# Thirty of the 32 query tiles of the last gate stage as three products of rounded parts

## The chip, the cores and the metric

The kernel runs on one core of a Trainium2 chip. The metric is device time in microseconds (us) of the whole program. Engines are named as in the profile: PE is TensorE's matmuls and PEld its weight loads, DVE is VectorE, ACT is ScalarE, POOL is GpSimd, SP is SyncE, which issues most of the DMA loads. A line such as L1227 is a line of the kernel before.

## The reference, cut to what matters

The program is a hybrid block (a gated delta rule, latent attention, a feed-forward part) followed by a second block with two layers of "product-key experts". In the last of these the 256 image tokens go through this:

```python
q = (hb @ w_q).reshape(PEER_BLOCK, PEER_HEADS, 2, PEER_DHALF)      # 1024 -> 8 heads x 2 x 256
s = jnp.einsum("nhkd,hkmd->nhkm", q, sub_keys)                     # 128 scores for each half
s_half, i_half = lax.top_k(s, PEER_TOPK)                           # 16 best of each half
cand = s_half[:, :, 0, :, None] + s_half[:, :, 1, None, :]         # 256 sums
top_s, top_c = lax.top_k(cand.reshape(..., 256), PEER_TOPK)        # 16 best pairs of a head
g = jax.nn.softmax(top_s, axis=-1)                                 # gates, then 16384 experts
```

`hb` is the input (1024 features by 256 tokens), `w_q` has 4096 output features: 32 tiles of 128, four for each head. All is float32.

## The kernel before

**Products.** TensorE multiplies float32 data in two ways here. A plain float32 product shows in the trace as two matmul records for each instruction of the program. The other way uses the type float32r: each operand is split into a high part (a copy rounded to that type) and a low part (the value less its high part), and three products high x high, high x low and low x high are summed in PSUM. Each of those is one record. The function `parted` (L682 to L692) does so for two earlier stages: ScalarE copies a 128x1024 tile of weights from the ring to a high buffer, VectorE subtracts it to make the low buffer (L2038), and the tensor engine multiplies 3 x 8 blocks (L688). The last gate stage before the change uses plain float32 products (L1227).

**The ring.** SyncE streams all weights through four SBUF slots of 128x1024 floats (512 KB each) in one fixed order. It refills a slot when the first matmul of a later slot has raised `slot_begun`; four loads at most are ahead. A consumer waits on `slot_loaded0` to `slot_loaded3`.

**The last gate stage** is `peer_last`, written once for each engine. Its order on each is as follows.
- VectorE scales the input (L2531), ScalarE shifts it (L1722) into `HT`, VectorE splits `HT` into high and low parts `HR` (L2542, L2543), which the expert sweep behind the stage needs.
- TensorE makes tile t of the queries into PSUM bank t % 2, eight blocks of 128x128 by 256 tokens (L1227). ScalarE copies it to SBUF (L1487 is the copy helper) and raises `lin_free`. After tile 4, 8, ... and at the end the tensor engine makes the scores of one head, `keys(h)`, 8 matmuls (L1212). `keys(h)` waits until VectorE has taken the scores of head h-2 (`key_scores_used`).
- VectorE takes each head's scores through `choice`: top 16 of each half (L2376 to L2380), the sums of pairs (L2393), top 16 of them, and the decoding of the indices (L2404 to L2418). After head 7 come the softmax (ScalarE L1770, VectorE L2451 to L2453), whose end raises `chosen`.
- Behind `keys(7)` TensorE works ahead on the first products of the expert sweep (L1025). It turns the choice (L1145) when `chosen` is raised, and then builds the gates in 32 groups (L1136) with VectorE (L2549 to L2553), ScalarE (L1777) and further work ahead (L1025) beside it. The expert sweep (L1045, L1047, L1059) follows.
- GpSimd waits for the split input, stores the residual to HBM (`park`, L420), waits for that, copies `HT` into the place of the residual (`unpark`, L425), waits, and has no more to do until near the end of the sweep.

Of the kernel before, what the change touches and what calls it, by code (L numbers as in the profile page):

```python
# [70 lines left out]
for _name, _w in (("in", 56), ("uq", 6), ("kn", 2), ("v", 2), ("o_gdn", 8), ("o_mla", 8), ("out", 8),  # L71
# [2 lines left out]
    SEGS[_name] = (_n, _w)  # L74
    _n += _w
NSLOTS = _n


def row_at(q):
# [63 lines left out]
def build(nc, io):  # L143
    ctx = ExitStack()
    with ctx:
# [23 lines left out]
        with nc.sbuf_tensor("arena_front", [P, 8192], F32):  # L169
            with nc.sbuf_tensor("wk_even", [P, 2, KD_, S], F32R) as t:  # L170
                WKL0, WKH0 = t[:, 0], t[:, 1]
                with nc.sbuf_tensor("wk_gap_a", [P, 2560], F32):
                    with nc.sbuf_tensor("wk_odd_low", [P, KD_, S], F32R) as t:
                        WKL1 = t[:, :, :]
                        with nc.sbuf_tensor("wk_gap_b", [P, 4608], F32):
                            with nc.sbuf_tensor("wk_odd_high", [P, KD_, S], F32R) as t:
                                WKH1 = t[:, :, :]
                                with nc.sbuf_tensor("text_low_a", [P, 4, S], F32R) as t:
                                    TLA = t[:, :, :]
                                    with nc.sbuf_tensor("wk_gap_c", [P, 2816], F32):  # L180
                                        with nc.sbuf_tensor("text_low_b", [P, 4, S], F32R) as t:
                                            TLB = t[:, :, :]
                                            with nc.sbuf_tensor("wk_gap_d", [P, 256], F32):
                                                with nc.sbuf_tensor("text_high", [P, KD_, S], F32R) as t:
                                                    TH = t[:, :, :]
# [227 lines left out]
        def _(pool):  # L413
# [4 lines left out]
            def park(dst, src, n):  # L418

                pool.dma_start(dst, src).then_inc(sem("x_parked"), 16)  # L420
                pool.wait_ge(sem("x_parked"), 16 * n)
# [98 lines left out]
            batch(io["cm"], 15)  # L520
            pool.wait_ge(sem("x_back"), 16 * (NH + 5))
            pool.wait_ge(sem("input_parts"), 4)
            park(parked[:, :, image], X[:, :, image], 5)
            unpark(INPUT, HT, NH + 6)
            pool.wait_ge(sem("coef_ready"), 3 * NEXP - 8)
            unpark(XT, parked[:, :, image], NH + 7)

# [79 lines left out]
        def _(pe):  # L607
# [3 lines left out]
            def arrived(w):  # L611
                pe.wait_ge(sem(f"slot_loaded{w % RING}"), 16 * (w // RING + 1))
# [420 lines left out]
            def split_experts(p):  # L1033

                n0, s0, e = NEXP * p, STEADY[p], AHEAD[p]
                if p:
                    L.take("input_parts")

                def up(j, b, first=False):

                    if not first:
                        pe.wait_ge(sem("sum_ready"), j + (s0 - e - 1))
                    pe.wait_ge(sem("u_low"), j + (s0 - e + 1))
                    for k in range(8):
                        mm(bank(b), SPL[b][:, 0, 0, P * k:P * k + P], HR[:, k, :, :], start=(k == 0), stop=False,  # L1045
                           skip_group_check=True)
                        last = mm(bank(b)[:, 0:S], SPL[b][:, 0, 1, P * k:P * k + P], HR[:, k, 0, :], start=False,  # L1047
                                  stop=(k == 7), skip_group_check=True)
                    last.then_inc(sem("up_ready"), 1)

                def down(j, b, first=False, opening=False):

                    parts = v_parts(j, b, opening)
                    pe.wait_ge(sem("coef_ready"), j + (n0 + 1))
                    pe.wait_ge(sem("v_low"), j + (n0 + 1))
                    for i in range(2):
                        for c, v in ((0, 0), (0, 1), (1, 0)):
                            for f in range(2):
                                last = mm(bank(2 + 2 * i + f), CFR[:, b, c, P * i:P * i + P],  # L1059
                                          parts[:, v, 512 * f:512 * f + 512],  # L1060
                                          start=(first and c == 0 and v == 0), stop=False, skip_group_check=True)
                    last.then_inc(sem("coef_used"), 1)

                if e:
                    pe.wait_ge(sem("gelu_done"), n0 + 10)
                    pe.wait_ge(sem("gates_evacuated"), n0 // 4 + 32)
                    for j in range(e):
                        if j == e - 1:
                            up(e, 0, True)
                        down(j, j % 2, j == 0, True)  # L1070
                    up(e + 1, 1, True)
                    down(e, 0)
                else:
                    up(0, 0, True)
                    up(1, 1, True)
                    pe.wait_ge(sem("gates_evacuated"), n0 // 4 + 32)
                    down(0, 0, True)
                with pe.Fori(0, (NEXP - 2 - e) // 2) as i:
                    for b in range(2):
                        up(i * 2 + (e + b + 2), b)  # L1080
                        down(i * 2 + (e + b + 1), 1 - b)
                down(NEXP - 1, 1)
# [116 lines left out]
            def peer_last():  # L1199

                l0 = L.lin

                def keys(h):

                    pe.wait_ge(sem("lin_free"), l0 + 4 * h + 4)
                    if h >= 2:
                        L.take("key_scores_used")
                    arrived(L.slots)
                    for k in range(2):
                        for i in range(2):  # L1210
                            for d in range(2):
                                last = mm(bank(2 + 4 * (h % 2) + i)[:, P * k:P * k + P],  # L1212
                                          QT[:, 4 * h + 2 * k + d, P * i:P * i + P],
                                          ring[:, L.slots % RING, P * (2 * k + d):P * (2 * k + d) + P],
                                          start=(k == 0 and d == 0), stop=(d == 1), skip_group_check=True)
                                if k == 0 and i == 0 and d == 0:
                                    last.then_inc(sem("slot_begun"), 1)
                    L.slots += 1
                    L.mark(last, "key_scores")

                for t in range(4 * NH):
                    pe.wait_ge(sem("lin_free"), l0 + max(t - 1, 0))
                    arrived(L.slots)
                    for k in range(8):
                        if t == 0:
                            L.take("inputs_shifted")
                        last = mm(bank(t % 2)[:, 0:S], ring[:, L.slots % RING, k * P:k * P + P], HT[:, k, :],  # L1227
                                  start=(k == 0), stop=(k == 7))
                        if k == 0:
                            last.then_inc(sem("slot_begun"), 1)  # L1230
                    last.then_inc(sem("lin_ready"), 1)
                    L.slots += 1
                    if t and t % 4 == 0:
                        keys(t // 4 - 1)
                keys(NH - 1)
                L.lin += 4 * NH
                beside = up_ahead(2)
                fill(beside, 32)
                for _ in range(2):
                    L.take("key_scores_used")  # L1240
                fill(beside, 12)
                turn_choice(KK)
                fill(beside, 9)
                L.take("chosen_evacuated")
                for n in range(32):
                    build(64 + n, n % 2, n < 2)
                    fill(beside, 1 if n % 3 == 2 else 2 if n < 31 else 8)
                sweep(2)
                turn_sums()
                L.take("acc_evacuated")  # L1250
                L.take("acc_evacuated")
# [232 lines left out]
        def _(act):  # L1484
# [244 lines left out]

            def queries():  # L1730

                def query(t, b, i=None):

                    n = L.lin + b + 1
                    act.wait_ge(sem("lin_ready"), n if i is None else i * 2 + n)
                    copy(QT[:, t, :], bank(b)[:, 0:S]).then_inc(sem("lin_free"), 1)

                query(0, 0)
                query(1, 1)
                with act.Fori(1, 2 * NH) as i:  # L1740
                    for b in range(2):
                        query(i * 2 + b, b, i)
                L.lin += 4 * NH
                act.wait_ge(sem("lin_free"), L.lin)

# [1226 lines left out]
```

## Time and profile before

| | us |
|---|---|
| median of 3 runs (4019.35 to 4029.62) | 4026.69 |
| the profiled execution | 4029.86 |
| its span, first to last instruction | 4027.9 |
| query tiles and first seven heads' scores | 3091.8 to 3217.0 |
| PE busy in the span | 3850.7 (96%) |
| DVE, ACT, POOL busy in the span | 2844.6, 1578.8, 88.1 |

The profile is of one execution. Its page has busy times by engine, the chain that ended last and the costliest groups; the trace behind it answers questions on one stretch, line or engine. A row of the timeline gives the start, the time that the instruction or the merged run of instructions took, the engine, line, operation and operands, and in brackets how long the engine was idle before it and what released it.

### The profile page before, as it was taken

To read this page: it belongs to the slowest core of one execution; us is meant where nothing else is said; L and a number is where in the kernel's file an instruction comes from. 1 tells how busy PE (TensorE), PEld (TensorE's weight loads), DVE (VectorE), ACT (ScalarE), POOL (GpSimd) and SP (SyncE) were. 2 spreads that over 40 slices of the span, in tenths; PEclk is the share of its full clock that TensorE was granted. 3 is DMA by queue.
4 is the path that set the end of the run, shared out by engine and by line. 5 is a ranking of instruction groups with operands and counts; after the bars stand their busy time and mean duration, and the time that the engine had idled before them with its cause. 6 is when DMAs were issued, how large, how long until landed. Compare 5 with 4: busy or idle time off the path is not lost.

```text
span 4027.9 us, 61202 instructions
## 1 busy us (share of the span) xinstructions
PE 3850.7 (96%) x21266; PEld 3190.8 (79%) x21266; DVE 2844.6 (71%) x5160; ACT 1578.8 (39%) x2416; POOL 88.1 (2%) x101
## 2 busy tenths in 40 slices
PE   7899899899999999999999999999969999999998
PEld 7697789554796888888888888888747888888887
DVE  6342356697598789999987777777562997777776
ACT  5201043132218544444475444444322084444443
POOL 0000000000000000000000000000400000000000
PEclk9899999899998999999999999999979999999999
DMA  5213255467424566666625666666765525666664
GB/s 191 63 48 106 93 174 168 161 224 236 141 96 135 178 196 191 195 191 190 198 89 162 188 188 188 189 190 193 174 208 168 168 68 184 189 190 188 188 188 145
DMA packets 203772, 666.51 MB, mean 165 GB/s; under 512 B 35920, under 2 KB 46176, under 8 KB 202480
## 3 DMA queue, kind: packets, MB, share of 16 engines
q1 hardware_dynamic: 166816, 602.71, 48.3%
q0 software_dynamic: 12496, 52.53, 4.2%
q10 hardware_dynamic: 24320, 9.37, 0.9%
q8 instruction: 91, 1.49, 0.2%
q14 instruction: 49, 0.40, 0.0%
HBM read 637.34 MB, written 26.15 MB: 165 GB/s over the span
## 4 chain that ended last, share of the span: by engine, by line
PE 91%; DVE 6%; DMA 2%; ACT 1%; issue 1%; SPq 0%; DVEq 0%; ACTq 0%; POOLq 0%
PE psum L1059 26%; PE psum L1045 17%; PE psum L1047 8%; PE psum L634 6%; PE psum L688 4%; PE psum L1136 4%; PE psum L712 4%; PE psum L1330 3%; PE psum L1227 3%; PE psum L1125 2%; PE psum L933 1%; PE psum L1025 1%; PE psum L1104 1%; DMA ring<-in_w 1%; PE psum L1400 1%
## 5 line engine op out<-in xcount | busy, mean ns | idle before, releaser
L1059 PE MATMUL psum<-rows_split_odd,coef_split 128*128 128x512 f32 x2400 | 590.9, 396 | 4.5 <-DVE rows_split_odd L2464 3.6
L1059 PE MATMUL psum<-rows_split,coef_split 128*128 128x512 f32 x2208 | 532.0, 390 | 0.3 <-issue 0.3
L2469 DVE TENSOR_REDUCE work<-psum 128x256 f32<-128x512 f32 x360 | 249.1, 692 | 400.6 <-PE psum L1047 399.5
L1059 PEld LDWEIGHTS psum<-rows_split_odd,coef_split 128*128 128x128 f32 x2400 | 437.9, 188 | 106.6 <-issue 6.7
L1045 PE MATMUL psum<-input_split,rows_split 128*128 128x512 f32 x1440 | 514.0, 397 | 1.2 <-DVE rows_split L2464 1.2
L1045 PE MATMUL psum<-input_split,rows_split_odd 128*128 128x512 f32 x1440 | 510.0, 393 | 0.0
L1680 ACT ACTIVATE work<-work 128x256 f32<-128x256 f32 x360 | 150.8, 419 | 875.6 <-DVE work L2469 875.6
L2464 DVE TENSOR_TENSOR rows_split_odd<-ring,rows_split_odd 128x1024 fp32r<-128x1024 f32 x380 | 462.6, 1218 | 5.9 <-ACT rows_split_odd L1487 5.9
L1059 PEld LDWEIGHTS psum<-rows_split,coef_split 128*128 128x128 f32 x2208 | 402.1, 188 | 81.4 <-issue 0.9
L1487 ACT ACTIVATE rows_split_odd<-ring 128x1024 fp32r<-128x1024 f32 x380 | 400.4, 1055 | 157.5 <-PE psum L1059 154.6
L2464 DVE TENSOR_TENSOR rows_split<-ring,rows_split 128x1024 fp32r<-128x1024 f32 x364 | 443.1, 1217 | 5.3 <-ACT rows_split L1487 5.3
L1487 ACT ACTIVATE rows_split<-ring 128x1024 fp32r<-128x1024 f32 x364 | 383.5, 1054 | 128.2 <-PE psum L1059 125.7
L1047 PE MATMUL psum<-input_split,rows_split_odd 128*128 128x256 f32 x1440 | 405.2, 281 | 0.0
L1047 PE MATMUL psum<-input_split,rows_split 128*128 128x256 f32 x1440 | 403.9, 280 | 0.0
L1487 ACT ACTIVATE arena<-psum 128x1024 f32<-128x1024 f32 (+6 forms) x209 | 176.9, 852 | 391.3 <-PE psum L1227 110.6
L1045 PEld LDWEIGHTS psum<-input_split,rows_split 128*128 128x128 f32 x1440 | 270.5, 188 | 66.1 <-ACT arena L1487 1.4
L1045 PEld LDWEIGHTS psum<-input_split,rows_split_odd 128*128 128x128 f32 x1440 | 270.4, 188 | 61.8
L1047 PEld LDWEIGHTS psum<-input_split,rows_split_odd 128*128 128x128 f32 x1440 | 271.5, 189 | 8.0
L1047 PEld LDWEIGHTS psum<-input_split,rows_split 128*128 128x128 f32 x1440 | 271.6, 189 | 6.9
L634 PE MATMUL psum<-arena,ring 128*128 128x256 f32 (+1 forms) x992 | 248.1, 409 | 6.5 <-DVE arena L2207 2.4
L634 PEld LDWEIGHTS psum<-arena,ring 128*128 128x128 f32 x992 | 189.0, 191 | 59.7 <-issue 28.4
L1136 PEld LDWEIGHTS psum<-work 128*128 128x128 f32 x1536 | 182.5, 194 | 49.7 <-issue 31.3
(447 smaller groups left out, 5296.2 us busy)
## 6 DMA issues: line engine op xcount, KB each, us to landing
ring<-in_u SPq DMA_DIRECT2D x384, 512.0 KB, 3.6
ring<-in_v SPq DMA_DIRECT2D x384, 512.0 KB, 3.5
ring<-in_w SPq DMA_DIRECT2D x372, 512.0 KB, 3.6
scratch_inj<-stage ACTq DMA_DIRECT2D x16, 512.0 KB, 5.5
arena<-scratch_inj POOLq DMA_DIRECT2D x7, 1024.0 KB, 7.7
scratch_cm<-work POOLq DMA_DIRECT2D x8, 512.0 KB, 6.2
scratch_cm<-arena POOLq DMA_DIRECT2D x8, 512.0 KB, 6.3
arena<-scratch_parked POOLq DMA_DIRECT2D x4, 1024.0 KB, 8.1
```

What stands on the lines that cost most here:

```text
L634: last = mm(bank(t % 2)[0:m, 0:n], ring[:, (w0 + s // 8) % RING, (s % 8) * P:(s % 8) * P + m], rhs[:, k, 0:n], start=(k == 0), stop=(k == ...
L688: last = mm(bank(t % 2)[:, 0:S], UPR[:, t % 3, w, P * k:P * k + P], UPI[:, k, x, :], start=(k == 0 and w == 0 and x == 0), stop=(k == 7 an ...
L712: ins = mm(bank(t % 2)[:, 0:S], ring[:, (w0 + s // 8) % RING, (s % 8) * P:(s % 8) * P + P], rhs[:, k, 0:S], start=(k == 0), stop=(k == kt ...
L1045: mm(bank(b), SPL[b][:, 0, 0, P * k:P * k + P], HR[:, k, :, :], start=(k == 0), stop=False, skip_group_check=True)
L1047: last = mm(bank(b)[:, 0:S], SPL[b][:, 0, 1, P * k:P * k + P], HR[:, k, 0, :], start=False, stop=(k == 7), skip_group_check=True)
L1059: last = mm(bank(2 + 2 * i + f), CFR[:, b, c, P * i:P * i + P], parts[:, v, 512 * f:512 * f + 512], start=(first and c == 0 and v == 0), s ...
L1136: last = mm(PS(1024 * b + P * t, P), EB[:, b, t, :], EA[:, b, t, :], start=(t % 4 == 0), stop=True, skip_group_check=True)
L1227: last = mm(bank(t % 2)[:, 0:S], ring[:, L.slots % RING, k * P:k * P + P], HT[:, k, :], start=(k == 0), stop=(k == 7))
L1487: copy = lambda o, i: f(o, i, ACT.Copy)
L1680: f(AC[:, b, :], AC[:, b, :], ACT.Gelu_apprx_tanh).then_inc(sem("gelu_done"), 1)
L2464: tt(parts[:, 1, :], ring[:, w % RING, :], parts[:, 0, :].bitcast(F32), ALU.subtract)\
L2469: dve.tensor_reduce(AC[:, b, :], bank(b).rearrange("p (x t) -> p t x", x=2), AX, ALU.add)\
```

## The change

Tiles 0 and 1 (`PLAIN` = 2) stay plain. For tiles 2 to 31 ScalarE copies the ring slot to the high half of one of three buffers `QW` (in regions of the arena that this stage does not use), GpSimd subtracts it from the slot to make the low half, and TensorE multiplies three times eight blocks with the split input `HR`. The high copy of tile t + 2 stands on ScalarE ahead of the copy of tile t out of PSUM; with three buffers it waits until tile t - 1 is done. TensorE waits for `input_parts` ahead of tile 2. On GpSimd the first two subtractions stand between the start of `park` and the wait for it, and the other 28 behind the start of `unpark`.

```diff
+QUERY_PARTS = QT_ - PLAIN + 1 + FT - PLAIN + 1 - PLAIN
+def query_slot(t):
+    return 4 * NEXP + SEGS["q1"][0] + t + max(0, (t - 1) // 4)
+def query_ring(t):
+    return query_slot(t) % RING
+def query_count(t):
+    return 16 * (query_slot(t) // RING + 1)
...
 # GpSimd
-            park(parked[:, :, image], X[:, :, image], 5)
-            unpark(INPUT, HT, NH + 6)
+            def query_low(t):
+                pool.wait_ge(sem("parts_high"), QUERY_PARTS + t + 1)
+                w = QW[t % 3]
+                pool.tensor_tensor(w[:, 1, :], ring[:, query_ring(t), :], w[:, 0, :].bitcast(F32), ALU.subtract)\
+                    .then_inc(sem("parts_low"), 1)
+            pool.dma_start(parked[:, :, image], X[:, :, image]).then_inc(sem("x_parked"), 16)
+            for t in range(PLAIN, 4):
+                query_low(t)
+            pool.wait_ge(sem("x_parked"), 80)
+            pool.dma_start(INPUT, HT).then_inc(sem("x_back"), 16)
+            for t in range(4, 4 * NH):
+                query_low(t)
+            pool.wait_ge(sem("x_back"), 16 * (NH + 6))
...
 # TensorE, peer_last
                 for t in range(4 * NH):
                     pe.wait_ge(sem("lin_free"), l0 + max(t - 1, 0))
-                    arrived(L.slots)
+                    if t >= PLAIN:
+                        pe.wait_ge(sem("parts_low"), QUERY_PARTS + t + 1)
+                    else:
+                        arrived(L.slots)
+                    if t == PLAIN:
+                        L.take("input_parts")
                     for k in range(8):
...
-                        last = mm(bank(t % 2)[:, 0:S], ring[:, L.slots % RING, k * P:k * P + P], HT[:, k, :],
-                                  start=(k == 0), stop=(k == 7))
+                        for w, x in ((0, 0), (0, 1), (1, 0)) if t >= PLAIN else ((0, 0),):
+                            first = k == 0 and w == 0 and x == 0
...
+                                last = mm(bank(t % 2)[:, 0:S], QW[t % 3][:, w, block], HR[:, k, x, :], start=first,
+                                          stop=(k == 7 and w == 1))
...
 # ScalarE, queries
+                def query_high(t):
+                    act.wait_ge(sem(f"slot_loaded{query_ring(t)}"), query_count(t))
+                    if t >= PLAIN + 3:
+                        act.wait_ge(sem("lin_ready"), L.lin + t - 2)
+                    copy(QW[t % 3][:, 0, :], ring[:, query_ring(t), :]).then_inc(sem("parts_high"), 1)
+                for t in range(PLAIN, PLAIN + 2):
+                    query_high(t)
+                for t in range(4 * NH):
+                    if PLAIN + 2 <= t + 2 < 4 * NH and t >= PLAIN:
+                        query_high(t + 2)
+                    act.wait_ge(sem("lin_ready"), L.lin + t + 1)
+                    copy(QT[:, t, :], bank(t % 2)[:, 0:S]).then_inc(sem("lin_free"), 1)
```

## Rows read from the trace of the kernel before

**Rows 1.** The page: shares of the span in the chain that ended last.

```profile
PE 91%; DVE 6%; DMA 2%; ACT 1%; issue 1%; SPq 0%; DVEq 0%; ACTq 0%; POOLq 0%
```

**Rows 2.** Timeline of ACT: copies of query tiles 0, 30 and 31.

```profile
3097.88 0.38 ACT L1487 ACTIVATE arena<-psum 128x256 f32<-128x256 f32 x1 [2.80 <-PE psum L1227]
...
3214.08 0.38 ACT L1487 ACTIVATE arena<-psum 128x256 f32 x1 [3.07 <-PE psum L1227]
3217.54 0.38 ACT L1487 ACTIVATE arena<-psum 128x256 f32 x1 [3.07 <-PE psum L1227]
```

**Rows 3.** Waits from 3080 to 3230: us in total, times, longest.

```profile
DVE arena L2376 <- PE psum L1212: 17.9, 7, 14.9
```

**Rows 4.** Timeline: first head's choice on DVE, and the scores on PE.

```profile
3113.54 0.89 DVE L2376 MAX8 arena<-psum 128x8 f32<-128x128 f32 x4 [14.88 <-PE psum L1212]
...
3118.94 0.69 DVE L2393 TENSOR_TENSOR arena<-arena 128x512 f32<-128x512 f32 x1
...
3124.01 0.18 DVE L2404 TENSOR_SCALAR arena<-arena 128x32 uint32<-128x32 uint32 x1
...
3124.91 1.22 DVE L2413 TENSOR_TENSOR arena<-arena,small 128x1024 f32<-128x1024 f32 x1
3126.16 1.22 DVE L2416 TENSOR_TENSOR arena<-arena 128x1024 f32<-128x1024 f32 x1
3127.42 1.22 DVE L2418 TENSOR_REDUCE arena<-arena 128x64 f32<-128x1024 f32 x1
3129.14 0.89 DVE L2376 MAX8 arena<-psum 128x8 f32<-128x128 f32 x4 [0.50 <-PE psum L1212]
...
3111.49 1.95 PE L1212 MATMUL psum<-ring,arena 128*128 128x128 f32 x16
```

**Rows 5.** Timeline: the end of the choice, and PE until it turns it.

```profile
3219.86 19.16 PE L1025 MATMUL psum<-X,ring 128*128 128x256 f32 x88
...
3222.30 0.89 DVE L2376 MAX8 arena<-psum 128x8 f32<-128x128 f32 x4
...
3238.97 0.42 DVE L2453 TENSOR_TENSOR arena<-arena,tail 128x256 f32<-128x256 f32 x1
...
3239.45 0.87 PE L1145 MATMUL psum<-small,arena 128*128 128x128 f32 x6 [0.43 <-DVE arena L2453]
```

**Rows 6.** Timeline of an earlier stage in three products (L688).

```profile
60.61 1.06 ACT L1487 ACTIVATE up_rows<-ring 128x1024 fp32r<-128x1024 f32 x1
...
62.31 0.47 ACT L1548 ACTIVATE arena<-psum,small 128x256 f32<-128x256 f32 x1 [0.64 <-PE psum L688]
...
65.19 0.47 ACT L1548 ACTIVATE arena<-psum,small 128x256 f32<-128x256 f32 x1 [0.70 <-PE psum L688]
```

**Rows 7.** Timeline of POOL and DVE where POOL's part begins.

```profile
3096.37 2.29 DVE L2543 TENSOR_TENSOR input_split<-arena,input_split 128x2048 fp32r<-128x2048 f32 x1
...
3099.21 0.85 POOL L420 DMA_DIRECT2D scratch_parked<-X  x1 [102.64 <-DVE input_split L2543]
...
3106.35 0.57 POOL L425 DMA_DIRECT2D X<-arena  x1 [6.29 <-DMA scratch_parked<-X]
```

**Rows 8.** POOL's memset of a 128x1024 tile: duration ns min/median/max.

```profile
L436 POOL MEMSET arena<- x4: 951/951/1024, 244.3 to 281.6; 128x1024 f32 x4
```

**Rows 9.** DVE beside POOL's DMA issues (L493): lines, then the timeline.

```profile
L2746 DVE TENSOR_SCALAR work<-work x7: 195/196/796, 2845.7 to 2854.4; 128x64 f32<-128x64 f32 x7
L2740 DVE TENSOR_TENSOR work<-work,tail x7: 224/224/226, 2844.5 to 2853.3; 128x64 f32<-128x64 f32 x7
...
2852.09 7.99 POOL L493 DMA_DIRECT2D arena<-scratch_lags  x7 [10.96 <-issue]
...
2852.44 0.80 DVE L2746 TENSOR_SCALAR work<-work 128x64 f32<-128x64 f32 x1
```

**Rows 10.** Stretches, us: busy PE, PEld, DVE, ACT, POOL, clock, DMA share, GB/s.

```profile
3091.00:3095.00 4.00, 3.22 (x8) 2.63 (x9) 2.29 (x7) 3.97 (x8) 0.00 (x0) 0.50 0.20 30
...
3260.00:3300.00 40.00, 37.84 (x283) 34.21 (x283) 37.88 (x60) 40.00 (x104) 0.00 (x0) 1.00 0.13 40
```

More of the change, by code:

```diff
@@ L171, in build @@
                 WKL0, WKH0 = t[:, 0], t[:, 1]
+                QW = [t[:, n].rearrange("p a b -> p (a b)").rearrange("p (w c) -> p w c", w=2) for n in range(2)]
                 with nc.sbuf_tensor("wk_gap_a", [P, 2560], F32):
@@ L174, in build @@
                         WKL1 = t[:, :, :]
+                        QW.append(t.rearrange("p a b -> p (a b)").rearrange("p (w c) -> p w c", w=2))
                         with nc.sbuf_tensor("wk_gap_b", [P, 4608], F32):
@@ L1035, in split_experts @@
                 n0, s0, e = NEXP * p, STEADY[p], AHEAD[p]
-                if p:
+                if p == 1:
                     L.take("input_parts")
@@ L1222, in peer_last @@
                     pe.wait_ge(sem("lin_free"), l0 + max(t - 1, 0))
-                    arrived(L.slots)
+                    assert L.slots % RING == query_ring(t)
+                    if t >= PLAIN:
[4 more added lines that the diff above has]
+                        L.take("input_parts")
                     for k in range(8):
@@ L1226, in peer_last @@
                             L.take("inputs_shifted")
-                        last = mm(bank(t % 2)[:, 0:S], ring[:, L.slots % RING, k * P:k * P + P], HT[:, k, :],
-                                  start=(k == 0), stop=(k == 7))
-                        if k == 0:
-                            last.then_inc(sem("slot_begun"), 1)
+                        block = slice(k * P, k * P + P)
+                        for w, x in ((0, 0), (0, 1), (1, 0)) if t >= PLAIN else ((0, 0),):
+                            first = k == 0 and w == 0 and x == 0
+                            if t < PLAIN:
+                                last = mm(bank(t % 2)[:, 0:S], ring[:, L.slots % RING, block], HT[:, k, :],
+                                          start=(k == 0), stop=(k == 7))
+                            else:
+                                last = mm(bank(t % 2)[:, 0:S], QW[t % 3][:, w, block], HR[:, k, x, :], start=first,
+                                          stop=(k == 7 and w == 1))
+                            if first:
+                                last.then_inc(sem("slot_begun"), 1)
                     last.then_inc(sem("lin_ready"), 1)
@@ L1730, in queries @@
             def queries():
[L1732 to L1742, printed above, removed]
+                def query_high(t):
[10 more added lines that the diff above has]
+                    copy(QT[:, t, :], bank(t % 2)[:, 0:S]).then_inc(sem("lin_free"), 1)
                 L.lin += 4 * NH
```

## The prediction

> **What bounds the kernel now.** I read the page's chain first: PE holds 91% of it [rows 1], so TensorE bounds the program as a whole. That says nothing about one stage, so I then read the stage by its waits and its timeline.
>
> Queries on TensorE: the copies of tiles 30 and 31 start 3.46 us apart [rows 2], so a plain tile takes 3.46 us. A head is four tiles and the scores' 1.8 us. Choice on VectorE: the first head starts at 3113.54, the second at 3129.14 after 0.50 us of idling [rows 4]; one head's choice therefore takes 3128.64 - 3113.54 = 15.10 us, in a period of 15.60 us. VectorE's seven waits for scores sum to 17.9 us, the first of them 14.9 [rows 3]: from the first head to the last it idles 3.0 us. Both engines are full, and what the next stage waits for is `chosen`, the end of VectorE's chain: 3238.97 + 0.42 = 3239.39 [rows 5]. TensorE fills the time after its last query with 19.16 us of work ahead and is idle only 0.43 us before it turns the choice [rows 5]. So the stage ends by two chains that are almost equally long. TensorE's cannot shorten it by more than VectorE's allows, and VectorE's is (start of the first choice) + 7 x 15.10 + (last choice and softmax, 3239.39 - 3222.30 = 17.09) + waits.
>
> **What is saved on TensorE.** An earlier stage with the same 24 matmuls a tile has its copies 65.19 - 62.31 = 2.88 us apart [rows 6]. Thirty tiles x (3.46 - 2.88) = 17.4 us. A head becomes 4 x 2.88 + 1.9 = 13.45 us, shorter than VectorE's 15.10. So all but a little of the 17.4 us turns into idling of TensorE at the end of its work ahead. What can reach the next stage is the 3.0 us of VectorE's waits and whatever the first choice gains at its start.
>
> **GpSimd's subtraction.** No row shows it. Its memset of the same tile, one stream of data, takes 0.95 us [rows 8], the low bound. Two reads and one write, all in turn, would be 3 x 0.95 = 2.85, the high bound. Two streams would be 1.90; I take 2.25, between two and three. The Trainium skill (GPSIMD Engine Reference, "Performance versus the Vector engine") gives 4497 ns for twice the size, half of which is 2.25 by that page; no row here shows it. At 2.25 GpSimd keeps up with 2.88. ScalarE's high copy is 1.06 us [rows 6] beside a copy of 0.38 [rows 2], so ScalarE keeps up too. After tile n is done, copy and high copy give the low part of tile n + 3 about 1.8 us later, ready 4.05 us after tile n; TensorE wants it 5.76 us after. That stays hidden. SP's loads go at 2.88 us a slot in the earlier stage [rows 6], so the ring is no new wait.
>
> **The start.** Tile 0 ends at about 3097.8 [rows 2], tile 1 at 3101.3. GpSimd waits for the split input, 3096.37 + 2.29 = 3098.66, and for the issue at 3099.21 of 0.85 us [rows 7]. Subtraction 2 then ends at 3102.3, subtraction 3 at 3104.6. Now it waits for the parked residual: the next issue starts at 3106.35 and takes 0.57 [rows 7], so subtraction 4 runs from 3106.9 to 3109.2. Tile 2 runs 3102.3 to 3105.2, tile 3 to 3108.1, tile 4 from 3109.2 to 3112.1, where the first scores start; before they started at 3111.49 [rows 4]. The first choice starts 0.6 us later, at 3114.15. With subtractions of 0.95 the store's wait remains and it is 0.7 earlier; with 2.85, 1.2 later.
>
> **GpSimd and VectorE in each other's way.** This is the largest term. Row: a VectorE operation of 0.20 us with one SBUF input took 0.80 beside GpSimd's DMA issues [rows 9]. It started at 2852.44 and ended at 2853.24; the first of seven issues in 7.99 us (1.14 each) that began at 2852.09 ended at 2853.23. VectorE stood still until GpSimd's instruction was over. VectorE's operations with two SBUF inputs kept 0.22 us [rows 9], but GpSimd read no tensor there. The subtraction reads two. I take it that it and VectorE's operations with two SBUF inputs exclude each other as whole instructions, and that the small one-input ones (from L2404) are held as in rows 9. The low bound is nothing; the high bound is that each of the 25 subtractions after the first choice's start holds VectorE for its full length, 25 x 2.25 = 56 us.
>
> The Trainium skill (SBUF — State Buffer, "Who interferes with whom") says that a VectorE instruction with two SBUF inputs contends with a GpSimd instruction that reads SBUF, and that the later one blocks fully. By that rule the sum is the one below; by the 0.22 us row alone it would lose most of this term.
>
> In a choice the exposed operations are the sums at offset 5.40 (0.69 us) and a group from offset 10.47 to 13.84: four small ones and two of 1.22 [rows 4]. Place the subtractions at 1.8 us after each tile's end and count, times from 3100:
> - Choice 0 starts 14.15, sums wanted 19.55. Subtraction 8 holds 18.75 to 21.0: 1.45 lost. The group wants 26.05; subtraction 10 ends 26.75: 0.7. Subtraction 11, ready at 27.4, gets in between two operations: 2.25. In all 4.4.
> - Choice 1 starts 33.65. Sums meet subtraction 14: 1.2. Subtractions 16 and 17 get in between operations of the group: 4.5. In all 5.7.
> - Choice 2 starts 54.5: 1.55, 0.75 and 2.2, in all 4.5.
> - By now TensorE is so far ahead that `keys(5)` waits for VectorE, and subtractions come later: choice 3 loses 1.1, choice 4 0.25, the rest none, since subtraction 31 is done in choice 4.
>
> Sum 15.95, call it 16, with 6 to 26 as the range of this count. Choice 7 then ends at 3114.15 + 105.7 + 16 + 17.1 = 3253.0.
>
> **TensorE's clock.** TensorE would finish its work ahead near 3233 and idle some 20 us. At the stage's opening it had idled 4.14 us and then had 0.50 of the clock, 1.2 GHz for 2.4, until tile 0 was out: 3091 to 3095 at 0.50 [rows 10], first copy at 3097.88 [rows 2]. Turning the choice took 0.87 us at full clock [rows 5]. About 6.8 us at half rate lose 3.4; in the gate building TensorE is busy 37.84 of 40 us and ScalarE 40.00 [rows 10], so little is regained. I take 2.5, from 0 to 4.
>
> **Sum.** +0.6 start, -3.0 waits, +16 exclusion, +2.5 clock = +16.1 us. The profiled execution's own time is 4029.86 (span 4027.9 and 1.96 around it), so it becomes 4046. That execution lies 3.2 us above the median of 4026.69; on the median's scale the forecast is 4043. A measurement of this kernel tells about 0.3%, 12 us, from no change: the three runs spread over 10.
>
> **Rivals.**
> 1. No exclusion between the subtraction and VectorE. For it: the 0.22 us row [rows 9]. Against: there GpSimd read nothing. The sum is +0.6 - 3.0 + 2.5 = +0.1, at most 4.7 us faster if the start and clock cost nothing: 4027 (4022 to 4031). This is the case on the other side, not slower; it decides if L2393, L2413 and L2416 keep their starts and lengths.
> 2. Only the small one-input operations are held. For it: L2746's row. GpSimd is busy 9.0 of 13.45 us; a group meets it with 0.67 x 1.12 = 0.75 us, and 0.9 us of small operations let another in with 0.27 x 2.25 = 0.6. Five heads x 1.35 = 6.7; in all +6.8: 4034.
> 3. The subtraction is dearer than its high bound, say 4 us, or its first call is slow, and GpSimd sets the pace. 30 x 4.0 + 3101 + the store's wait of 2 = 3223 for subtraction 31, last scores 3228, chosen 3245 without any exclusion; with 16 to 25 us of exclusion it is 3265: +20 to +35, 4055. For it: no row prices it. Against: memset at 0.95.
> 4. TensorE's 17 us arrive in full: 4009. Against: VectorE's 15.10 a head, which nothing shortens.
>
> **Chances.** Forecast 0.55 (its own range +8 to +28, 4035 to 4055), rival 1 0.16, rival 2 0.10, rival 3 0.17, rival 4 0.02. Over 12 us slower: 0.43 of the forecast's 0.55 and 0.16 of rival 3, 0.59. Within 12 us: 0.15 + 0.12 + 0.10 + 0.01 = 0.38. Faster: 0.03. The range leaves out a tenth on each side: 4021, the end of rival 1, to 4063, into rival 3.
>
> **What would show it.** Right: 24 matmuls a tile and 2.88 us between copies while nothing blocks; GpSimd subtractions of about 2.25; first choice at about 3114; choices 0 to 2 of 19 to 21 us with L2393, L2404 or L2413, L2416 stretched or delayed by up to 2.25, the last two 15.1; TensorE idle about 20 us before L1145 and at half clock after it. Wrong: choices of 15.1 throughout (rival 1), only L2404 to L2410 stretched (2), tiles over 3.4 us apart from the start (3). The sizes hang on where the subtractions fall among VectorE's operations, and on who goes first when both wait.

## The result and the profile after

The changed kernel takes 4048.59 us (median of 6, 4037.39 to 4063.25), the kernel before 4023.02 in the same comparison (median of 6, 4016.83 to 4029.62). The ratio is 1.0064 with a 95% interval of 1.0050 to 1.0078: 26 us slower, 20 to 31 by the interval. The execution profiled is the longest of the six, with a span of 4061.3 us, 33.4 above the span before. Of these, 4.6 us lie ahead of the stage, in code that is the same in both: the stage opens (ScalarE's eight normalizations) at 3095.66 instead of 3091.03. In the nine profiled executions (before, after and the seven experiments) that opening moves from 3082 to 3096, and what lies behind the stage takes 692.6 to 694.3 us, so everything below is counted from the opening. The table is worked out from the timelines of both kernels.

| us from the stage's opening | before | after | difference |
|---|---|---|---|
| first choice starts on VectorE | 22.51 | 27.50 | +5.0 |
| seven periods from choice to choice | 108.76 | 130.14 | +21.4 |
| last choice and softmax, to `chosen` | 17.09 | 17.08 | 0 |
| `chosen` to the start of the next expert sweep | 94.28 | 96.66 | +2.4 |
| sum | 242.64 | 271.38 | +28.7 |

Lines of the changed kernel for those of before: MAX8 L2423 (L2376), sums L2440 (L2393), small operations L2451 to L2457 (L2404 to L2410), the two products and the reduction L2460, L2463, L2465 (L2413, L2416, L2418), scores L1243 (L1212), work ahead L1056 (L1025), turning the choice L1176 (L1145). New are the matmuls of three products L1271 and GpSimd's subtraction L545.

The page's chain of the changed kernel answers to [rows 1]: VectorE has two points more, TensorE three fewer.

```profile
PE 88%; DVE 8%; DMA 2%; ACT 1%; issue 1%; SPq 0%; DVEq 0%; ACTq 0%; POOLq 0%
```

The waits of the changed kernel from 3080 to 3300 (us in total, times, longest) answer to [rows 3]. `wk_even` and `wk_odd_low` are the buffers `QW` of the split weights.

```profile
ACT wk_even L1531 <- DMA ring<-in_w: 43.1, 20, 8.0
...
ACT wk_odd_low L1531 <- DMA ring<-in_w: 23.5, 9, 7.3
...
DVE arena L2423 <- PE psum L1243: 19.9, 1, 19.9
...
PE psum L1056 <- DVE arena L2440: 11.4, 1, 11.4
...
PE psum L1176 <- DVE arena L2500: 3.9, 1, 3.9
```

VectorE now waits for scores once, before its first choice; the other six waits of [rows 3], 3.0 us, are gone. New is that ScalarE waits for weights in the ring, 29 times.

The timeline of the changed kernel from the opening to the first choice, beside [rows 4] and [rows 7]:

```profile
3103.83 0.85 POOL L548 DMA_DIRECT2D scratch_parked<-X  x1 [104.30 <-DVE input_split L2590]
3104.72 2.41 POOL L545 TENSOR_TENSOR wk_odd_low<-ring,wk_odd_low 128x1024 fp32r<-128x1024 f32 x1
...
3110.69 0.59 POOL L552 DMA_DIRECT2D X<-arena  x1 [1.21 <-DMA scratch_parked<-X]
3111.30 2.40 POOL L545 TENSOR_TENSOR wk_even<-ring,wk_even 128x1024 fp32r<-128x1024 f32 x1
...
3113.85 3.10 PE L1271 MATMUL psum<-input_split,wk_even 128*128 128x256 f32 x24 [0.64 <-POOL wk_even L545]
3118.02 1.06 ACT L1531 ACTIVATE wk_odd_low<-ring 128x1024 fp32r<-128x1024 f32 x1 [7.26 <-DMA ring<-in_w]
3118.98 0.37 ACT L1531 ACTIVATE arena<-psum 128x256 f32<-128x256 f32 x1
...
3119.40 3.65 PE L1243 MATMUL psum<-ring,arena 128*128 128x128 f32 x16 [2.44 <-ACT arena L1531]
```

Read it from the end. The first scores started when ScalarE had copied out query tile 3 (3118.98). That copy stood behind the high copy of tile 5 (3118.02), which had waited 7.26 us for tile 5's weights. The loads of the ring, the 1 MB store of the residual (issued at 3103.83) and the 1 MB return (3110.69) are under way together here. The load of tile 5's weights was issued at 3110.64, just ahead of the return, and the two took this long from issue to landing (KB, us):

```profile
X<-arena POOLq DMA_DIRECT2D x1, 1024.0 KB, 7.6
ring<-in_w SPq DMA_DIRECT2D x1, 512.0 KB, 7.4
```

The start has a second part. TensorE had idled 2.44 us before the scores and made them with half the clock (the stretch from 3120 to 3122; columns as in [rows 10]):

```profile
3120.00:3122.00 2.00, 2.00 (x11) 2.00 (x11) 0.00 (x0) 0.89 (x2) 2.00 (x2) 0.50 0.35 43
```

They took 3.65 us for the 1.95 of [rows 4]. So of the +5.0 us, 3.3 are scores that start later against the opening (23.74 for 20.46) and 1.7 are scores made at the lower clock.

The timeline of the first choice after the change, against [rows 4]:

```profile
3127.88 2.40 POOL L545 TENSOR_TENSOR wk_odd_low<-ring,wk_odd_low 128x1024 fp32r<-128x1024 f32 x1 [0.34 <-ACT wk_odd_low L1531]
...
3128.56 2.26 DVE L2440 TENSOR_TENSOR arena<-arena 128x512 f32<-128x512 f32 x1
...
3134.10 4.83 POOL L545 TENSOR_TENSOR wk_even<-ring,wk_even 128x1024 fp32r<-128x1024 f32 x2 [3.83 <-ACT wk_even L1531]
...
3135.20 1.31 DVE L2451 TENSOR_SCALAR arena<-arena 128x32 uint32<-128x32 uint32 x1
...
3136.54 2.43 DVE L2453 TENSOR_SCALAR arena<-arena 128x32 uint32<-128x32 uint32 x1
...
3139.47 1.23 DVE L2460 TENSOR_TENSOR arena<-arena,small 128x1024 f32<-128x1024 f32 x1
3139.66 3.29 POOL L545 TENSOR_TENSOR wk_odd_low<-ring,wk_odd_low 128x1024 fp32r<-128x1024 f32 x1 [0.72 <-ACT wk_odd_low L1531]
...
3140.73 3.31 DVE L2463 TENSOR_TENSOR arena<-arena 128x1024 f32<-128x1024 f32 x1
...
3144.07 1.22 DVE L2465 TENSOR_REDUCE arena<-arena 128x64 f32<-128x1024 f32 x1
```

The sums (0.69 us in [rows 4]) were issued at 3128.56 and recorded until 3130.82; the subtraction that was already running ended at 3130.28. The two small operations ended at 3136.51 and 3138.97, which is the end of the first and of the second of the two subtractions from 3134.10 to 3138.93: the second subtraction got in between two VectorE operations that follow each other, and an operation of 0.18 us took 2.43. The subtraction at 3139.66 lasted 3.29 us instead of 2.40, since L2460 was running until 3140.70; then L2463, issued at 3140.73, had to wait for that subtraction to end (3142.95) and ended 1.1 us after it. So the recorded duration of a held operation holds its wait, and each engine holds the other. The reduction, 1.22 us beside a subtraction, was not held. Added up, choice 0 lost 1.57 + 1.13 + 2.25 + 2.08 = 7.0 us.

The lines of VectorE's operations after the change, 3085 to 3260 (ns min/median/max):

```profile
L2440 DVE TENSOR_TENSOR arena<-arena x8: 691/692/2836, 3128.6 to 3258.7; 128x512 f32<-128x512 f32 x8
...
L2453 DVE TENSOR_SCALAR arena<-arena x7: 181/181/2432, 3136.5 to 3248.9; 128x32 uint32<-128x32 uint32 x7
L2457 DVE CAST arena<-arena x7: 195/195/2385, 3139.2 to 3249.3; 128x64 f32<-128x64 uint32 x7
...
L2463 DVE TENSOR_TENSOR arena<-arena x7: 1224/3303/3310, 3140.7 to 3250.8; 128x1024 f32<-128x1024 f32 x7
L2465 DVE TENSOR_REDUCE arena<-arena x7: 1220/1220/1222, 3144.1 to 3252.0; 128x64 f32<-128x1024 f32 x7
```

By the groups' means over this stretch, the excess over the shortest duration is L2463 8.3 us, L2453 4.4, L2440 3.7, L2451 3.5, L2457 2.2, L2460 2.1: 24.2 us. That is all but 0.2 us of what the periods gained over 15.1 (22.16, 18.47, 21.42, 20.61, 17.22, 15.12, 15.14: 7.1, 3.4, 6.3, 5.5, 2.1, 0, 0).

The end of the stage after the change, on TensorE's timeline and in two stretches of 2 and 4 us (busy PE, PEld, DVE, ACT, POOL, clock, DMA share, GB/s), against [rows 5] and [rows 10]:

```profile
3232.78 15.29 PE L1056 MATMUL psum<-X,ring 128*128 128x256 f32 x64
3259.49 7.02 PE L1056 MATMUL psum<-X,ring 128*128 128x256 f32 x24 [11.42 <-DVE arena L2440]
3270.44 1.54 PE L1176 MATMUL psum<-small,arena 128*128 128x128 f32 x6 [3.93 <-DVE arena L2500]
...
3270.00:3272.00 2.00, 1.56 (x7) 1.56 (x8) 0.38 (x1) 0.00 (x0) 0.00 (x0) 0.50 0.00 0
3272.00:3276.00 4.00, 4.00 (x10) 3.14 (x10) 3.88 (x6) 1.86 (x6) 0.00 (x0) 0.50 0.01 2
```

TensorE idled 11.42 + 3.93 = 15.4 us before it turned the choice, and did that and the next 4 us at half clock: 1.54 us for what took 0.87 at full clock [rows 5].

### The profile page after: what moved, and what is told of

Same layout as the page of the kernel before. It is cut to its first block, busy times and chain, and to the rows that moved or that the text cites. A ratio compares the mean times of both kernels' runs of the same rounds, so it can differ in the third digit from the quotient of the medians.

```text
span 4061.3 us, 61679 instructions
## 1 busy us (share of the span) xinstructions
PE 3854.5 (95%) x21506; PEld 3203.2 (79%) x21506; DVE 2867.7 (71%) x5160; ACT 1609.9 (40%) x2446; POOL 164.8 (4%) x131
## 4 chain that ended last, share of the span: by engine, by line
PE 88%; DVE 8%; DMA 2%; ACT 1%; issue 1%; SPq 0%; DVEq 0%; ACTq 0%; POOLq 0%
PE psum L1090 26%; PE psum L1076 16%; PE psum L1078 8%; PE psum L665 6%; PE psum L719 4%; PE psum L1167 4%; PE psum L743 4%; PE psum L1374 3%; PE psum L1156 2%; PE psum L1056 1%; PE psum L964 1%; DMA ring<-in_w 1%; PE psum L1135 1%; PE psum L1444 1%; PE psum L1455 1%
## 5 line engine op out<-in xcount | busy, mean ns | idle before, releaser
L1531 ACT ACTIVATE arena<-psum 128x1024 f32<-128x1024 f32 (+5 forms) x209 | 176.8, 851 | 300.0 <-PE psum L1156 86.2
```

The source lines that it names most:

```text
L1531: copy = lambda o, i: f(o, i, ACT.Copy)
```

## The experiments

Each is told by its ratio to the kernel before, run on the same chip at the same time, and by the difference of its stage (opening to the next sweep) from the 242.64 us of before. In three of them GpSimd's work is changed alone; four move work.

**GpSimd stops after tile 4.** Its theory: without the subtractions beside VectorE the choices go back to 15.1 us, and the late start and the clock stay.

```diff
-            for t in range(4, 4 * NH):
-                query_low(t)
+            query_low(4)
 # TensorE, before a tile's matmuls
-                        pe.wait_ge(sem("parts_low"), QUERY_PARTS + t + 1)
+                        pe.wait_ge(sem("parts_low"), QUERY_PARTS + min(t, 4) + 1)
+                        pe.wait_ge(sem("parts_high"), QUERY_PARTS + t + 1)
```

> GpSimd subtracts for tiles 2 to 4 only; tiles 5 to 31 are multiplied with the low parts that stand in the buffers from those three (so their own low parts are left out), with 24 matmuls each and the same high copies, loads, store and return. Theory (GpSimd's subtraction and VectorE's operations with two SBUF inputs or in the small one-input form exclude each other): all of VectorE's choices take 15.1 us; the first starts as late as in the changed kernel (5.0 us later than before), 3.0 us of waits are gone, TensorE's clock costs 2.3, sum +4 us on the kernel before (0.1%). Rival (the late ring loads and ScalarE's order are what stretches the stage): about as slow as the changed kernel, +20 to +25 us.

Measured: 4026.05 us (median of 10), ratio 1.0012 (0.9997 to 1.0028). The stage is +4.8: first choice at 27.71 us, all seven periods 15.14, `chosen` to sweep 96.71. The sums, the second product and a small one (ns min/median/max):

```profile
L2440 DVE TENSOR_TENSOR arena<-arena x8: 691/692/694, 3119.5 to 3225.4; 128x512 f32<-128x512 f32 x8
...
L2463 DVE TENSOR_TENSOR arena<-arena x8: 1224/1225/1227, 3126.7 to 3233.4; 128x1024 f32<-128x1024 f32 x8
...
L2453 DVE TENSOR_SCALAR arena<-arena x8: 180/181/183, 3124.8 to 3231.5; 128x32 uint32<-128x32 uint32 x8
```

All three products a tile, ScalarE's high copies and idling of TensorE (5.91 and 3.87 us before it turns the choice) are still there; the 24 us are not. They come from GpSimd's instructions alone. The late first choice does not come from those after tile 4; here too the load of tile 5 was waited for (7.61 us), and the scores took 3.51 us.

**GpSimd writes as long, and reads nothing.** Two memsets of free columns, 1383 + 955 ns on average, stand where each subtraction from tile 5 on stood.

```diff
-            for t in range(4, 4 * NH):
-                query_low(t)
+            query_low(4)
+            for t in range(5, 4 * NH):
...
+                pool.memset(A(16896, 1536), 0.0).then_inc(sem("spare"), 1)
...
+                pool.memset(A(16896, 1024), 0.0).then_inc(sem("parts_low"), 1)
```

> As the first experiment, but for each tile from 5 on GpSimd fills 1536 and then 1024 columns of a free region with zeros (about 1.4 and 0.95 us, near the 2.4 us of the subtraction), reading nothing; tiles 5 to 31 leave out their own low parts. Theory (what excludes is the read side for two-input operations, either side for the small ones): L2440, L2460 and L2463 keep 0.69 and 1.23 us, L2451 to L2457 are held now and then, some 1.3 us a head over five heads; +4 and +6 = +10 us on the kernel before. Rival (any work of GpSimd holds VectorE's two-input operations): like the changed kernel, +22 to +28 us. Second rival (nothing is held by writes): +4 us.

Measured: 4035.18 us (median of 5), ratio 1.0049 (1.0031 to 1.0066). The stage of the profiled execution is +7.1, the lost time in its choices 6.5. Here L2445 is the sums, L2458 and L2460 are small ones, L2465 and L2468 the products:

```profile
L2445 DVE TENSOR_TENSOR arena<-arena x8: 691/692/693, 3118.9 to 3231.3; 128x512 f32<-128x512 f32 x8
...
L2458 DVE TENSOR_SCALAR arena<-arena x8: 181/182/978, 3124.2 to 3237.3; 128x32 uint32<-128x32 uint32 x8
L2460 DVE CAST arena<-arena x8: 194/195/1477, 3124.4 to 3237.6; 128x64 f32<-128x64 uint32 x8
...
L2468 DVE TENSOR_TENSOR arena<-arena x8: 1224/1224/1226, 3126.1 to 3239.3; 128x1024 f32<-128x1024 f32 x8
```

Against a GpSimd that only writes, no operation with two SBUF inputs is held, and the small one-input ones are, by up to the length of a memset. The Trainium skill (SBUF — State Buffer, "Who interferes with whom") states both halves: two SBUF inputs contend only with a GpSimd instruction that reads, `cast` and `tensor_scalar` can contend through their two-port modes, `tensor_reduce` never does. By that rule, the traces agree: 1224 to 1226 ns here and up to 3310 beside the subtraction, 1220 to 1222 for the reduction. The timed difference is larger than the 7 us of the stage: 20 us by the ratio, 15 by the medians (4020.33 for the kernel before), above the 10 that the theory expected and near the rival's 22 to 28. What decides against the rival is the length of L2468, not the total. The rest of the gap is not explained. It lies neither in the profiled execution's stage nor behind it (694.3 us, as before). TensorE's mean granted clock was lower than before, 0.9728 for 0.9752, but in the experiment before this one it was 0.9727 and the timed difference no more than its stage.

**The subtractions alone.** The kernel before, with 25 subtractions of the same size on free columns beside its choices; query tiles stay plain.

```diff
+            pool.tensor_tensor(A(16896, 4, S), HT[:, 0:4, :], HT[:, 4:8, :], ALU.subtract).then_inc(sem("spare"), 1)
+            for t in range(8, 4 * NH):
+                pool.wait_ge(sem("lin_ready"), 204 + t - 2)
+                pool.wait_ge(sem("spare"), t - 7)
+                pool.tensor_tensor(A(16896, 4, S), HT[:, 0:4, :], HT[:, 4:8, :], ALU.subtract).then_inc(sem("spare"), 1)
...
```

> The kernel before, its query products untouched, with 25 subtractions of 128x1024 on GpSimd beside them (operands of no use to the result, written to a free region), one for each finished tile from tile 5 on. Theory: the exclusion alone stretches the choices, about 4 to 5 us in each of heads 0 to 5, 25 us in all; the 3.0 us of waits absorb their part, an idle TensorE behind its work ahead costs 2 us of clock; +22 to +26 us on the kernel before, with the first choice at its old place. Rival (loads and ScalarE's order): nothing of them is changed here, so 0 to +3 us.

Measured: 4034.64 us (median of 7), ratio 1.0036 (1.0017 to 1.0055), +14 us. The stage is +15.0: start -0.3, 18.1 us lost in five choices, 3.0 of it back from VectorE's former waits. `chosen` to the sweep took 94.3 us as before, so the 2 us of clock that were expected did not come (TensorE idled 2.53 us before it turned the choice). The sums, a small one (ns min/median/max) and the second product (us busy, mean ns of one, us idle before):

```profile
L2401 DVE TENSOR_TENSOR arena<-arena x8: 691/718/2780, 3119.3 to 3243.4; 128x512 f32<-128x512 f32 x8
L2412 DVE TENSOR_SCALAR arena<-arena x8: 180/270/2071, 3124.6 to 3249.2; 128x32 uint32<-128x32 uint32 x8
...
L2424 DVE TENSOR_TENSOR arena<-arena 128x1024 f32<-128x1024 f32 x8 | 17.9, 2241 | 0.3
```

The exclusion needs nothing else of the change. It fell short of what was expected, since a subtraction that comes with each plain tile, 3.46 us apart, meets VectorE elsewhere: L2424 lost 8.1 us, L2401 4.3, L2412 5.7, the rest nothing.

**The store and the return moved back.** The changed kernel; GpSimd issues the store of the residual behind the subtraction of tile 12 and the return behind that of tile 18.

```diff
-            pool.dma_start(parked[:, :, image], X[:, :, image]).then_inc(sem("x_parked"), 16)
...
-            pool.wait_ge(sem("x_parked"), 80)
-            pool.dma_start(INPUT, HT).then_inc(sem("x_back"), 16)
...
+                if t == 12:
+                    pool.dma_start(parked[:, :, image], X[:, :, image]).then_inc(sem("x_parked"), 16)
+                if t == 18:
+                    pool.wait_ge(sem("x_parked"), 80)
+                    pool.dma_start(INPUT, HT).then_inc(sem("x_back"), 16)
```

> The changed kernel with one edit: the store of the residual is issued behind subtraction 12 and its return behind subtraction 18, not at the start. Theory (the first scores come late because ScalarE's copy of tile 3 stands behind the high copy of tile 5, whose ring load waits in the same DMA queues as the store and the return): the first choice starts 6.6 us sooner against the stage's start than in the changed kernel, 1.7 sooner than before, and the kernel is 6 to 7 us faster than the changed one, about +19 us on the kernel before. Rival (the delay is hidden by what the choices lose later): no faster than the changed kernel, +25 us.

Measured: 4041.04 us (median of 4), ratio 1.0055 (1.0033 to 1.0077). The first choice starts at 21.38 us, 6.1 sooner than in the changed kernel and 1.1 sooner than before. Its timeline (opening at 3088.61):

```profile
3106.19 1.06 ACT L1531 ACTIVATE wk_odd_low<-ring 128x1024 fp32r<-128x1024 f32 x1 [3.43 <-DMA ring<-in_w]
3107.16 0.36 ACT L1531 ACTIVATE arena<-psum 128x256 f32<-128x256 f32 x1
...
3107.94 1.95 PE L1243 MATMUL psum<-ring,arena 128*128 128x128 f32 x16
```

The load that it waited for, from issue to landing:

```profile
ring<-in_w SPq DMA_DIRECT2D x1, 512.0 KB, 3.5
```

The same copy waits 3.43 us for its weights instead of 7.26, TensorE no longer waits for ScalarE before the scores, and it makes them at full clock, in 1.95 us for 3.65. The copy starts 4.8 us earlier against the opening (17.58 for 22.36): 3.9 because its load took 3.5 us and not 7.4, and 0.9 because that load was issued sooner. So the late start was made mainly by the transfer beside the load. The expectation above puts them in the same queues; the profile has the ring's loads in q1 and the store and the return in q0, and what they have in common is the DMA engines, 0.87 busy from 3110 to 3118 in the changed kernel. The rest is the ring itself: with the store later, ScalarE still waits 26 times for it, 55.8 us in all, where the earlier stage of [rows 6] has no such wait.

The choices still lose 17.4 us (periods 17.20, 16.22, 20.34, 18.35, 20.78): with other meetings the loss is another, 17 instead of 24. The stage is +15.4, half of the change's 28.7: 6.1 us of the difference are the start, 7 the meetings. In the timed runs the gain is not clear of noise (1.0033 to 1.0077 against 1.0050 to 1.0078).

**Three versions that keep out of VectorE's way.** The first splits 23 tiles and lets GpSimd subtract only when VectorE has passed a given point; the second splits nine, the last six subtractions after the sums of a head; the third splits 24 and gives GpSimd also the second product (L2463's) of seven heads, its reduction following in the next head's choice. All three also issue the store behind their first three to six subtractions.

```diff
 # 23 tiles
+            for h in range(NH - 1):
+                if h:
+                    pool.wait_ge(sem("head_chosen"), NH + h)
+                    query_low(4 * h + 6)
+                    query_low(4 * h + 7)
+                if h < NH - 2:
+                    pool.wait_ge(sem("key_scores_used"), NH + h + 1)
+                    query_low(4 * h + 8)
...
 # nine tiles
+            for h in range(NH - 2):
+                pool.wait_ge(sem("key_scores_used"), NH + h + 1)
+                query_low(4 * h + 8)
...
 # 24 tiles and the product
+                pool.tensor_tensor(OH, OH, over(IDF.rearrange("p m i a -> p (m i) a"), 16, 2), ALU.mult)\
+                    .then_inc(sem("product_zeroed"), 1)
...
```

> Twenty-three tiles in three products (2 to 4, then the second, third and fourth of each head's four, 30 and 31); the store is issued behind subtraction 7, the return later. GpSimd waits for VectorE: two subtractions start at the end of a choice, the third when the sums of pairs (L2440) are made, so that all fall into the 5.4 and 4.3 us in which VectorE has no exposed operation. Theory (exclusion depends on where the subtractions fall): choices 15.1 us each, exposed operations at 0.69, 0.18, 0.20 and 1.23 us, first choice 1.7 us sooner than before, chosen 4.5 us sooner; TensorE idles some 8 us behind its work ahead and pays 2.3 of clock: 2 us faster than before, -4 to +2. Rival (GpSimd's subtractions slow VectorE in any position): 23 of them cost 15 us and more.

> Only nine tiles in three products: 2, 3 and 4 ahead of the first choice, with the store behind their subtractions, and the last tile of six heads, its subtraction started when L2440 is done. Theory (VectorE's chain is the bound, and its slack is 3.0 us of waits and what the first choice gains): first choice 1.7 us sooner, a head 15.1 us instead of 15.6, chosen 4.7 us sooner, TensorE idle about 1 us and its clock kept, so 4 to 5 us faster than the kernel before (0.11%). Rival (the products themselves are the stage's bound, 0.58 us for each tile): 5.2 us of matmul time saved, about the same; the two part in the fifth experiment, where the rival would give 13 us.

> Twenty-four tiles in three products, and GpSimd also takes over one of VectorE's operations of heads 0 to 6: the weighing of the one-hot rows (L2463), whose sum over them VectorE makes behind L2440 of the next head. Subtractions are placed where VectorE has no exposed operation. Theory (both chains must get shorter for the stage to end sooner): VectorE's head 13.85 us, TensorE's 13.9, the first choice 1.7 us sooner; chosen 11 to 13 us sooner, TensorE hardly idle: 9 to 13 us faster than the kernel before (0.25 to 0.3%). Rival (GpSimd's three streams cost VectorE more than they relieve it of): no faster than before.

| version | median us (12 runs each) | ratio to before (29 runs) | stage |
|---|---|---|---|
| 23 tiles, gated | 4020.86 | 0.9990 (0.9974 to 1.0006) | -0.7 |
| nine tiles | 4024.98 | 0.9992 (0.9979 to 1.0006) | -3.4 |
| 24 tiles, product on GpSimd | 4023.31 | 0.9994 (0.9981 to 1.0007) | -4.2 |

The sums and the second product of the version with 23 tiles, then the second product with nine:

```profile
L2451 DVE TENSOR_TENSOR arena<-arena x8: 691/693/2699, 3112.4 to 3221.5; 128x512 f32<-128x512 f32 x8
L2474 DVE TENSOR_TENSOR arena<-arena x8: 1224/1225/1226, 3119.7 to 3229.5; 128x1024 f32<-128x1024 f32 x8
```

```profile
L2468 DVE TENSOR_TENSOR arena<-arena x8: 1224/1225/1226, 3129.8 to 3237.1; 128x1024 f32<-128x1024 f32 x8
```

Placement takes the loss from 24 us to 2.6 with 23 subtractions, 20 of them issued behind the first choice's start where the change has 25, and to nothing with the nine tiles (six there). Then the stage has what the prediction said was there at most: the 3.0 us of waits and a little at the start. Moving 1.22 us of VectorE's 15.1 a head to GpSimd was to give 8 more and gave 0.8 over the nine tiles. Half of what was missed is exclusion again: two small operations lost 4.5 us (means of 471 and 473 ns for 181 and 196). The waits of that version show the other half:

```profile
ACT wk_even L1543 <- DMA ring<-in_w: 36.6, 15, 5.4
ACT wk_odd_low L1543 <- DMA ring<-in_w: 23.7, 8, 4.0
...
DVE arena L2436 <- PE psum L1254: 17.8, 3, 13.3
```

VectorE waits for scores again, 4.4 us after the first, and the scores wait for ScalarE's copies, which stand behind high copies that wait for weights. Its periods are 15.24, 15.62, 16.12, 14.66, 14.72, 14.59, 13.87. No version is measurably faster than before; each interval holds 1.

## Why the prediction came out as it did, point by point

| term of the sum | predicted | measured in the stage |
|---|---|---|
| start | +0.6 | +5.0 |
| VectorE's waits | -3.0 | -2.9 |
| exclusion | +16 (6 to 26) | +24.2 |
| clock | +2.5 | +2.4 |
| sum | +16.1 | +28.7 |

- **What bounds the stage.** VectorE's chain does: the choices of 15.1 us take up every saving on TensorE. Right; with GpSimd's subtractions left out from tile 5 on and all 30 tiles in three products the periods were 15.14 each and the stage +4.8, though TensorE saves its 17.4. With nine to 24 tiles split the stage changed by -0.7 to -4.2 us, where TensorE saves 5 to 14.
- **Subtraction 2.25 us.** 2.34 to 2.46 where nothing held it, 2.54 and 2.62 on average in the stage. The Trainium skill (GPSIMD Engine Reference, "Performance versus the Vector engine") gives 4497 ns for twice the size; the measured 2.40 is 7% above half of it. Rival 3, a subtraction of 4 us, is out: the forecast's high bound of 2.85 was not reached by one that nothing held.
- **Exclusion.** The mechanism was right in both its parts, operations with two SBUF inputs and the small one-input ones. What failed is the size, in the step "place the subtractions at 1.8 us after each tile's end and count": counted 4.4, 5.7, 4.5, 1.1, 0.25, measured 7.1, 3.4, 6.3, 5.5, 2.1. The subtractions came later and less evenly, since ScalarE's high copies waited for ring loads (29 waits, 66.6 us). They met more operations of choices 0, 3 and 4, and held one for 2.0 us or more nine times, where the prediction counts four such meetings. Subtractions at other places cost 17.4 (store moved), 18.1 (alone) and 2.6 us (gated): the count of meetings is the term, and made on the profile of before it was 8 us off.
- **Start.** The step that failed is "so the ring is no new wait". It was taken from an earlier stage with loads at 2.88 us a slot [rows 6], which has no store and no return of 1 MB beside them and never waits for the ring. The high copy of tile 5 waited 7.26 us, since its load took 7.4 us beside the return, and ScalarE works in order, so tile 3 came out late. Tile 4 was on time: TensorE ended it at 3116.95, which is 3112.3 against the opening of before, where 3112.1 was forecast; but the scores started 2.4 us after it and not at once. They also met half the clock, 1.7 us that the prediction counts only for the end of the stage. In the two other runs with this order of the first transfers the first choice started at 27.71 and 24.81 us (the scores took 3.51 and 2.05), so the term is +2.3 to +5.2; with the store later it is -1.1.
- **Clock.** TensorE idled 15.4 us instead of the 20 forecast, and had half the clock after it: 1.54 us for [rows 5]'s 0.87. Predicted 2.5, measured 2.4; 2.4 also with the subtractions gone.
- **Rivals.** Rival 1 (no exclusion) and rival 2 (only small operations) fell with L2440 and L2463 at up to 2.8 and 3.3 us. Rival 2 is what a GpSimd that only writes does: 6.5 us, against the 6.7 of its sum; that the sizes agree so well is luck, since the sum counts five heads with 1.35 each and the run had three with 1.3 to 3.6. Rival 4 fell with the run that leaves the subtractions out, where TensorE had its saving and the stage gained nothing.
- **The working.** The sum holds together. Two slips change nothing: 4 x 2.88 + 1.9 is 13.42 and not 13.45, and the "about 1.8 us" for copy and high copy is 1.44 by its own rows (0.38 + 1.06); the 0.4 between them comes from no row.

The forecast of 4043 us for the median stands against 4048.59, and by the comparison's ratio +26 against +16: the errors of two terms, +4.4 and +8.3, add up to 12.6 in the stage. That the total is only 5.6 off is in part luck: the kernel before was 3.7 us faster in the comparison than in the runs that the forecast starts from, and the timed difference (26) is a little under the profiled stage's 28.7.

## What to carry to other kernels

Work given to GpSimd is not free when VectorE bounds the stage: count the VectorE operations with two SBUF inputs and the small casts and `tensor_scalar`s that each GpSimd instruction can meet, and price a meeting at up to the GpSimd instruction's whole length (here 2.4 us on an operation of 0.2). If the work must be there, let a semaphore that VectorE raises place it where VectorE reads PSUM or searches. Before a copy is put ahead of another on an in-order engine, look for what else the DMA engines move at that time, not only for the rate of a quiet stage: one load took 7.4 us for 3.5.

## What the runs showed of the hardware that was not expected

- A GpSimd instruction can start between two VectorE operations that follow each other 0.03 us apart: L2453 of 0.18 us took 2.43. Each gap in a row of short operations is a place where this can happen.
- The exclusion works both ways: a subtraction of 2.40 us took 3.29 and 3.39 beside the two products, and 2.37 to 2.40 beside searches and MAX8.
- A GpSimd memset holds TENSOR_SCALAR and CAST of 32 to 64 columns (to 1.48 us) and leaves 1024 columns of two-input work alone (1224 to 1226 ns).
- Runs of one kernel differ along with TensorE's mean granted clock: over the 29 runs of before on the chip of the last three versions (4011 to 4033 us), a line through time and mean granted clock gives 2.8 us for 0.001 (correlation -0.91). The line does not carry over from kernel to kernel: two experiments with the same mean clock, 0.973, stood 5 and 20 us above the kernel before, with stages of +4.8 and +7.1. Differences of 3 us in a stage can be read in its timeline, and not in the total.
